# Third mixer of a diffusion-transformer kernel: the sink logits are written on VectorE ahead of the scores

## What is computed

```python
s = jnp.where(valid, jnp.einsum('bqhgd,bkhd->bhgqk', qi, kb).astype(jnp.float32), neg)
s_ctx = jnp.einsum('bqhgd,bkhd->bhgqk', qi, kc).astype(jnp.float32)
s_sink = jnp.broadcast_to(sink_l[None, :, :, None, None], s.shape[:-1] + (1,))
p = softmax_f32(jnp.concatenate([s, s_ctx, s_sink], axis=-1), v.dtype)
return (jnp.einsum('bhgqk,bkhd->bqhgd', p[..., :span], vb)
        + jnp.einsum('bhgqk,bkhd->bqhgd', p[..., span:span + C], vc))
```

## Time and profile before

| | |
|---|---|
| median of 3 runs | 2345.12 us (2344.96 to 2345.4) |
| profiled execution, its own time | 2343.62 us |
| its span, first to last instruction | 2341.8 us |
| mean granted TensorE clock | 0.998 |
| busy: TensorE / VectorE / ScalarE / GpSimd | 98% / 60% / 43% / 20% |
| mixer C, sequence units | about 401 to 455 us and 979 to 1032 us |

### The profile page before, as it was taken

One profiled execution on the slowest core, in us unless ns is written; L12 is line 12 of the kernel. 1 busy time (PEld: TensorE's weight loads), 2 busy tenths in 40 slices (PEclk: granted clock), 3 DMA queues, 4 the chain that ended last, 5 costly groups with the idle time before them and its releaser, 6 DMA issues.

```text
span 2341.8 us, 39975 instructions
## 1 busy us (share of the span) xinstructions
PE 2300.3 (98%) x15942; PEld 1902.9 (81%) x15942; DVE 1401.3 (60%) x2818; ACT 1011.9 (43%) x1750; POOL 464.9 (20%) x291
## 2 busy tenths in 40 slices
PE   8999999999999999999999999999999999999998
PEld 7878878788888888888887688888888768888887
DVE  5878776787136766453388558847857755333333
ACT  5773375723247527653455442222235535221221
POOL 2102212022441131214752420000014232000001
PEclk9999999999999999999999999999999999999999
DMA  7303413042222151112241125445442112323222
GB/s 308 143 2 145 171 47 127 2 189 98 67 92 78 59 198 57 55 64 90 86 157 62 56 91 198 167 148 185 170 142 82 55 54 90 100 78 112 99 83 70
DMA packets 64201, 250.51 MB, mean 107 GB/s; under 512 B 7408, under 2 KB 9968, under 8 KB 54544
## 3 DMA queue, kind: packets, MB, share of 16 engines
q1 hardware_dynamic: 61216, 236.10, 29.0%
q0 software_dynamic: 2592, 11.54, 1.5%
q10 hardware_dynamic: 208, 0.33, 0.0%
HBM read 243.67 MB, written 4.19 MB: 106 GB/s over the span
## 4 chain that ended last, share of the span: by engine, by line
PE 89%; ACT 4%; DVE 3%; issue 2%; DVEq 1%; DMA 1%; POOL 1%; ACTq 0%; SPq 0%
PE ps L2948 41%; PE ps L2744 13%; PE ps L2729 8%; PE ps L2925 6%; PE ps L621 4%; PE ps L730 4%; ACT probs L937 3%; PE ps L671 3%; PE ps L715 1%; PE ps L2758 1%; PE ps L2965 1%; PE ps L2615 1%; DMA stage_low<-in_ada 1%; DVEq L820 1%; PE ps L2781 1%
## 5 line engine op out<-in xcount | busy, mean ns | idle before, releaser
L2948 PE MATMUL ps<-h_split,split_panels 128*128 128x512 f32 x2088 | 500.0, 394 | 1.2 <-ACT projected L1788 0.8
L2948 PEld LDWEIGHTS ps<-h_split,split_panels 128*128 128x128 f32 x2088 | 387.9, 188 | 92.8 <-issue 14.7
L1251 POOL TENSOR_TENSOR split_panels_first<-panels_first,split_panels_first 128x1024 fp32r<-128x1024 f32 (+2 forms) x100 | 220.8, 2208 | 728.9 <-ACT split_panels_first L1468 728.9
L2744 PE MATMUL ps<-h_split_first,split_panels_first 128*128 128x256 f32 (+1 forms) x1680 | 294.4, 337 | 0.0
L2744 PEld LDWEIGHTS ps<-h_split_first,split_panels_first 128*128 128x128 f32 x1680 | 258.3, 190 | 34.3 <-issue 1.0
L1269 POOL TENSOR_TENSOR probs_turned<-probs_turned,probs 128x512 f32<-128x512 f32 x30 | 40.0, 1332 | 764.3 <-ACT probs L1731 761.7
L2729 PE MATMUL ps<-h_split_first,split_panels_first 128*128 128x512 f32 (+1 forms) x900 | 190.5, 370 | 0.9 <-POOL h_split_first L1290 0.9
L2729 PEld LDWEIGHTS ps<-h_split_first,split_panels_first 128*128 128x128 f32 x900 | 156.3, 189 | 32.4 <-issue 3.0
L2243 DVE TENSOR_TENSOR split_panels<-panels,split_panels 128x1024 fp32r<-128x1024 f32 (+2 forms) x110 | 127.7, 1164 | 89.0 <-ACT split_panels L1493 88.9
L1920 ACT ACTIVATE probs<-ps 128x512 f32<-128x512 f32 x44 | 26.3, 599 | 349.8 <-PE ps L2948 349.7
L1493 ACT ACTIVATE split_panels<-panels 128x1024 fp32r<-128x1024 f32 (+2 forms) x149 | 144.7, 979 | 67.0 <-PE ps L2948 63.0
(11 more groups left out here) (341 smaller groups left out, 3964.7 us busy)
## 6 DMA issues: line engine op xcount, KB each, us to landing
panels<-in_w SPq DMA_DIRECT2D x88, 512.0 KB, 3.7
modulation_panels<-in_ada SPq DMA_DIRECT2D x40, 1024.0 KB, 4.9
panels_first<-in_in SPq DMA_DIRECT2D x72, 512.0 KB, 4.8
late_modulation_panel<-in_ada SPq DMA_DIRECT2D x24, 1024.0 KB, 4.8
panels<-in_in SPq DMA_DIRECT2D x42, 512.0 KB, 3.7
panels_first<-in_out SPq DMA_DIRECT2D x32, 384.0 KB, 3.1
panels<-in_w SPq DMA_DIRECT2D x32, 384.0 KB, 3.5
panels<-in_w SPq DMA_DIRECT2D x32, 320.0 KB, 2.9
```

Source lines behind the costliest of these rows:

```text
L1251: nc.gpsimd.tensor_tensor(flat1(n, 1)[:, s], raw1[:, n % RAW1, s], flat1(n, 0)[:, s].bitcast(F32), ALU.subtract).then_inc(rest1_done, 1)
L2744: ins = mm(to, split1[:, s, w, c, :], hs1[:, h, c, lo:lo + n], start=c == 0 and i == 0, stop=c == KC - 1 and i == 2)
L2948: ins = mm(out, panel_of(n, l)[:, a, c - base, :], moving(b, c), start=first and i == 0 and j == 0, stop=last and i == len(chunks) - 1 and ...
```

## The change

For a sequence unit with i of 2 or more (`sinks_ahead`), the sinks are no longer written behind its scores. VectorE writes them one step earlier: after the third-bank copy of `prev`, whose banks the coming unit will get, it waits for the ScalarE copy of `prev`, drains, writes the two sink columns of the coming unit, drains, and only then takes the reciprocal for `prev`. Before the scores of such a unit TensorE now waits also for the `weight_ready` of the unit that held the banks, which that reciprocal raises. The two units i = 0, 1 and the context units keep the order of before.

```diff
--- before.py
+++ after.py
@@ -609,6 +609,9 @@
                 pe.wait_ge(pt_by_act, u["banks_of"]["events"][0]["c"] + 1)
             elif u["banks_of"]:
                 pe.wait_ge(exp_done, 2 * u["banks_of"]["u"] + 2 + o.u * 2)
+            if sinks_ahead(u):
+
+                pe.wait_ge(weight_ready, u["banks_of"]["u"] + 1 + o.u)
             last = {}
             third = u["banks_of"]["events"][1:] if u["banks_of"] and u["in_sets"] else []
             for e, col, a, z in segments(u):
@@ -800,10 +803,8 @@
             if "band" in u:
                 n, kind = u["band"]
                 dve.wait_ge(band_in[kind], 16 * (n + 1))
-            if "sink" in u:
-                for e in range(2):
-
-                    V.tensor_copy(scores_at(u, e, u["w"][e])[:, u["w"][e] - 1:], sinks[:, u["sink"] + e:u["sink"] + e + 1])
+            if "sink" in u and not sinks_ahead(u):
+                sinks_dve(u)
                 dve.drain()
             if u["mask"] == "last tile":
                 for e in range(2):
@@ -837,6 +838,15 @@
                     V.tensor_tensor_reduce(out=S, in0=S, in1=mask, scale=sign, scalar=HIGHEST, op0=ALU.add,
                                            op1=ALU.min, accum_out=row_min[:, s:s + 1]).then_inc(max_ready, 1)
 
+        def sinks_ahead(u):
+
+            return "sink" in u and u["i"] >= 2 and len(u["tiles"]) > 2
+
+        def sinks_dve(u):
+
+            for e in range(2):
+                nc.vector.tensor_copy(scores_at(u, e, u["w"][e])[:, u["w"][e] - 1:], sinks[:, u["sink"] + e:u["sink"] + e + 1])
+
         def turned_dve(dve, u, o):
 
             for ev in u["events"]:
@@ -897,6 +907,13 @@
                         behind_first()
                 if prev:
                     turned_dve(dve, prev, o)
+                    coming = next((x["unit"] for x in plan if x["unit"] and x["unit"]["i"] == u["i"] + 1), None) if u else None
+                    if coming and sinks_ahead(coming):
+
+                        dve.wait_ge(pt_by_act, prev["events"][0]["c"] + 1)
+                        dve.drain()
+                        sinks_dve(coming)
+                        dve.drain()
                     weights_dve(dve, prev, o)
                 values_dve(dve, step, o, halves=True)
                 if u and step["values_first"]:
```

## The result

The change made the kernel slower: 2350.62 us in the median of 10 runs (2348.81 to 2353.07) against 2345.02 (2343.48 to 2346.25), ratio 1.0026 with a 95% interval of 1.0018 to 1.0034. That is 5.6 us; the forecast was 7.2 us, 2352.3. The profiled execution has a span of 2348.8 us (2341.8 before). The mean granted clock is 0.997 (0.998 before).

What follows compares the result with a forecast made beforehand. TensorE, 98% busy, was taken as bound by a loop of hand-overs in the third mixer. A period of 15.17 against 14.17 us gave +3.62 per layer, +7.2 in all: 2345.12 to 2352.3 us, range 2348.2 to 2356.5.

Steps and rivals of the forecast that it cites:

- The loop: Third mixer: stalled scores delay turning, its ScalarE copy and VectorE's work before the next scores; TensorE stalls about 0.55 us.
- The tail, 0.71 us: From ScalarE copy's end to scores: hand-over 0.04, first drain 0.13, sinks and second drain 0.34, reciprocal 0.16, hand-over 0.04.
- The disputed drain: First new drain on VectorE, of unknown cost: between 0 and 0.24 us; the skill's price is about 12 ns.
- d: Length of the first drain ahead of the sinks, taken as 0.13 us: 0.11 of issue and 0.02 for the drain.
- The four steps: One four-unit period of the third mixer, turning to turning: 15.17 us against 14.17 before, +1.00 us.
- T: Start of the turning matmuls of `prev` in a step, from which the forecast counted its times.
- VectorE last in one step of four: Five-tile `prev`, 641-column `u`: VectorE's third-bank copy ends at T + 2.09, behind the ScalarE copy at T + 1.91; step 3.84.
- Over the stage: Whole mixer stage: +0.40 us to the first delayed turning, +3.22 to unit 14's; 3.62 per layer, nothing behind hiding it.
- The break-even tail: Rival of a gain, tail hidden behind TensorE's outputs: needs under about 0.46 us; faster or within 0.2%, 7%.
- The gain if the sinks were free: Sinks leave the path to the minima, nothing put in place: about 0.34 us x 3.5 periods x 2 layers, 2.4 us.
- The heavier tail: Rival: first drain of 0.24 us or more and sink copies not overlapping; 2355.3 us, or 2358.0 with 0.10 more; 13%.
- its second reading of the drain: By the skill, a next VectorE operation waits for an empty pipe, so sink copies don't overlap: 0.10 us longer, 2355.0.

Runs made afterwards that it cites:

- dve_stall_only: Changed kernel with the sinks back behind the scores and TensorE's new wait removed; VectorE keeps its wait for ScalarE and both drains: 2347.07 us, 1.0010 of the kernel before.
- pe_wait_only: Changed kernel with the sinks back behind the scores and VectorE's wait and drains removed; TensorE keeps its wait for `weight_ready`: 2345.22 us, 1.0007 of the kernel before.
- twice: Changed kernel with a second pair of sink copies and a third drain ahead of the reciprocal: 2360.53 us, 1.0069 of the kernel before.
- own_signal: Changed kernel, but the second sink copy signals the scores, reciprocal behind it, first drain before the ScalarE wait, second drain gone: 2343.84 us, 0.9994 of the kernel before.
- late_only: Changed kernel with TensorE's wait for `weight_ready` moved behind the first scores matmul of the first head: 2347.78 us, 1.0014 of the kernel before.
- early_signal: Changed kernel with the reciprocal ahead of the ScalarE wait, the second sink copy raising `weight_ready`, second drain gone: 2344.78 us, 1.0000 of the kernel before.
- no_sinks: Changed kernel with no sinks written for units 2 to 15 and no waits for them, leaving out part of the softmax: 2341.71 us, 0.9989 of the kernel before.
- pe_sinks: Kernel before, with TensorE writing each sink column as a one-column matmul behind each head's scores, VectorE's sinks and drain gone: 2356.80 us, 1.0050 of the kernel before.

## Why the prediction was right

**The loop.** Forecast: scores, turning, ScalarE copy, tail, scores, in three steps of four; TensorE stalls behind L865 by 0.5 to 0.6 us. Measured: 14 such stalls in a layer, 8.0 us, mean 0.57. That the tail closes a loop through TensorE's scores was right. The way round it was right in two steps of four only: I had the loop pass VectorE's own minima in one step and turning and ScalarE copy in three, and it was the reverse. dve_stall_only and pe_wait_only show that neither wait does it alone, twice that added tail is paid in full, and own_signal that a short tail pays nothing.

**The tail, 0.71 us.** At 430.06 the ScalarE copy ends (429.05 + 1.01), at 430.77 the scores start: 0.71. Its parts were mis-sized against each other. Hand-over and first drain took 0.10 (forecast 0.17), sinks and second drain 0.30 (0.34), and the reciprocal with the hand-over to TensorE 0.31 (0.20). The disputed drain shows in the queue's rows of line 914:

```profile
L914 DVEq DRAIN  x28: 19/124/338, 404.2 to 1032.9; - x28
```

Where VectorE has nothing in flight it lasts 19 ns, so with the 0.04 of issue behind it d was 0.06, nearer its lower bound than the 0.13 that I took. The Trainium skill ("VectorE: DVE Perf Modes", section "The DRAIN you can't avoid") gives its 12 ns to the boilerplate drains at a program's start and end; that row's 19 ns is near it, though the section has no price for a drain that a kernel writes. By it the tail would have been 0.59 against 0.71 measured. Its sum of 2349.0 lies as near to 2350.6 as 2352.3 does, because other terms were off as well. What it lacked is in the hand-over from the reciprocal to TensorE, 0.14 and not 0.04 (chain view: the part named issue between the reciprocal and the scores):

```profile
415.31 0.16 DVE ps L848
415.48 0.06 DVEq L916
415.54 0.07 issue
415.61 0.18 DVE row_weight L865
415.78 0.14 issue
415.92 1.40 PE ps L624 x16
```

Most of this 0.14 is not VectorE's. Several semaphores are waited for in front of these scores, and the trace has an instruction of its own in TensorE's queue that takes up the waits for `pt_by_act` and `weight_ready`, 0.11 before each of the 14 scores of a layer (in front of those at 419.71 it starts at 419.6):

```profile
L614 PEldq EVENT_SEMAPHORE  x14: 51/51/51, 404.8 to 453.4; - x14
```

late_only has its wait for `weight_ready` alone, on a later matmul and with no such instruction, and there the same reciprocal is 0.04 from TensorE:

```profile
418.76 0.18 DVE row_weight L867
418.94 0.04 issue
418.99 1.39 PE ps L626 x12
```

0.10 us in each of 28 tails that are on the loop is 2.8 us, half of what the change lost. It is an estimate from these rows: no run takes away this instruction alone.

**The four steps.** Forecast 3.81, 3.84, 3.71, 3.81; measured 3.80 (417.09 to 420.89), 3.85, 3.58, 3.63: 15.17 against 14.86. Three terms were mis-sized, and partly cancel; that the first two steps came out to 0.01 is luck. First, the time from scores to turning: I took 1.31, 1.08 and 1.09 from rows where TensorE had not been stalled; behind a stall it was 1.18, 0.95 and 0.95 (419.71 to 420.89, 423.79 to 424.74, 427.37 to 428.32), 0.13 to 0.14 less each time, 0.5 us per period. Second, the ScalarE copy started 0.03 to 0.05 sooner after T (417.09 to 417.83 is 0.74, where I took 0.78), 0.12 in the three steps that I summed through it. Third, I had VectorE last in one step of four. It was in three: the minima started 0.25 after T (417.09, 417.34) instead of 0.14, and the sinks then waited for them or for the third-bank copy. That gave back 0.16, 0.14 and 0.04 in the first three steps, 0.34 per period. Together that is the 0.31 between 15.17 and 14.86. The first and the third are two sides of one thing: the minima start 1.42 us after the scores do, as before (415.92, 417.34), while turning has moved closer to the scores.

**Over the stage.** 2.5 us per layer instead of 3.62, all from the step lengths; that the second layer is like the first, and that nothing behind hides it, held.

**The rivals.** The break-even tail was forecast as 0.46 us. early_signal has that tail where ScalarE is last, and ran level with the kernel before, its period 0.16 shorter; own_signal, with 0.37 from sinks to scores, under it. The gain if the sinks were free was forecast as 2.4 us; no_sinks measured 2.5 by medians and 1.1 per layer in the stage; per period 0.35, where I had 0.34. The heavier tail and its second reading of the drain fell: the two copies overlap, 0.22 for two of 0.16. The section of the Trainium skill that the prediction cites for the opposite ("VectorE: DVE Perf Modes", "The DRAIN you can't avoid") says itself that a next operation that is not held starts earlier, so the trace need not disagree with it.

## What to carry to other kernels

Work moved out of one hand-over lands in another; before moving it, ask which engine's wait it will stand behind and whether that wait is already the loop. If it must stand in a loop, let the instruction that others wait for raise the semaphore itself, put nothing in front that the waiting engine does not need (here a reciprocal and a drain), and place the consumer's wait at the first instruction that needs it, apart from its other waits: the same early write went from 0.26% slower to 0.11% faster (interval 0.02% to 0.20%) by these three. And look at the chain again after such a change: here the loop moved to another engine, and only the tail that both ways round share made the forecast hold.

## What the runs showed of the hardware

TensorE's hand-over from a ScalarE exponential is 0.04 to 0.05 us, and that from a VectorE reciprocal 0.04 too where the matmul itself waits for it (418.94 in late_only). Where the wait is in a semaphore instruction of 0.05 us in front of the matmul, the hand-over is 0.14 (415.78). Behind a stall the turning starts 0.13 us sooner after the scores than without one; why, no run settles. In late_only the turning even starts before the last scores matmul, as if matmuls on the two halves of the rows went ahead of each other:

```profile
412.73 0.27 PE L676 MATMUL ps<-matrices,probs 64*128 64x64 f32 x1
412.75 0.27 PE L626 MATMUL ps<-qkv 64*128 64x128 f32 x1
```

L676 is the turning, L626 the scores, which the program has first; so the order of the recorded starts is not always the program's. A one-column matmul on a 128 x 128 float32 stationary costs 0.27 us in pe_sinks (0.54 for two). Each is recorded as two weight loads of 0.19 and two passes of 0.25; which of the two sets the pace no run shows:

```profile
L635 PEld LDWEIGHTS ps<-minus_sinks,matrices x160: 186/190/192, 395.9 to 1042.5; 128*128 128x128 f32 x160
L635 PE MATMUL ps<-minus_sinks,matrices x160: 250/250/271, 395.9 to 1042.6; 128*128 128x1 f32 x160
```
